# Two transformer blocks in one kernel: operands before squares at the seam, and two units evicted ahead of the norm's root

## The reference

```python
# first_block, its end
h2 = rmsnorm(x, norm_ffn)
gate, up = jnp.split(h2 @ w_ffn_in, 2, axis=-1)
x = x + (jax.nn.silu(gate) * up) @ w_ffn_out          # w_ffn_out: 2816 x 1024
x = rmsnorm(x, norm_final)
# second_block, its start
a = rmsnorm_2(x, norm_pre_mix)
proj = a @ w_in                                        # 1024 x 1960
...                                                    # gates, mLSTM, latent attention
mix = ...
x = x + rmsnorm_2(mix, norm_post_mix)                  # x is needed again here
```

## Time and profile before

| | us |
|---|---|
| median of 3 runs | 2873.16 |
| lowest and highest | 2871.89, 2873.46 |
| the profiled execution | 2871.33 |
| its span | 2869.6 |
| TensorE's mean granted clock in it | 0.986 |

### The profile page before, as it was taken

The page is one execution under the profiler, slowest core; times in us unless marked ns, Lnnn a source line. Parts: engine busy times, 40 slices in busy tenths (PEclk is TensorE's granted clock), DMA queues, the critical chain, the costliest instruction groups (busy, mean ns, idle before and its releaser), DMA issues.

```text
span 2869.6 us, 32978 instructions
## 1 busy us (share of the span) xinstructions
PE 2764.7 (96%) x12578; PEld 2186.6 (76%) x12578; DVE 1812.8 (63%) x2070; ACT 1021.9 (36%) x1397; POOL 1277.2 (45%) x780
## 2 busy tenths in 40 slices
PE   6999999999998999999998999999998999999998
PEld 5888688787776888887786887666577688878777
DVE  3111355655746766669878758666646766687877
ACT  4000233333214333334444014555545433344444
POOL 2433222223435888884333434101432788833331
PEclk9999999999999999999999999999799999999999
DMA  5222232324442333346631534002343355564543
GB/s 178 95 95 91 102 112 94 118 89 157 144 139 66 111 108 94 90 125 211 203 114 48 185 118 123 17 32 79 104 132 103 103 162 158 160 218 161 159 135 132
DMA packets 336967, 348.90 MB, mean 122 GB/s; under 512 B 18915, under 2 KB 256602, under 8 KB 336822
## 3 DMA queue, kind: packets, MB, share of 16 engines
q1 hardware_dynamic: 327254, 311.30, 35.2%
q10 hardware_dynamic: 9568, 35.66, 3.1%
HBM read 237.53 MB, written 108.34 MB: 121 GB/s over the span
## 4 chain that ended last, share of the span: by engine, by line
PE 78%; DVE 11%; issue 3%; DMA 3%; ACT 3%; POOL 1%; SPq 1%; DVEq 0%; ACTq 0%; POOLq 0%
PE ps L3264 34%; PE ps L532 29%; PE ps L2352 2%; PE ps L2374 2%; DVE op_lo L3341 2%; PE ps L939 1%; PE ps L2722 1%; DMA op_raw<-hidden 1%; PE ps L2362 1%; DVE sw_lo L3174 1%; PE ps L920 1%; PE ps L574 1%; PE ps L873 1%; PE ps L568 1%; PE ps L2840 1%
## 5 line engine op out<-in xcount | busy, mean ns | idle before, releaser
L3264 PE MATMUL ps<-op_hi,sw_hi 128*128 128x512 f32 x1769 | 693.5, 392 | 21.9 <-ACT s_p L3273 9.1
L3264 PE MATMUL ps<-op_lo,sw_hi 128*128 128x512 f32 x1769 | 690.2, 390 | 0.0
L3264 PE MATMUL ps<-op_hi,sw_lo 128*128 128x512 f32 x1769 | 690.1, 390 | 0.0
L498 POOL TENSOR_TENSOR w_hi_t<-w_raw,ones 128x1024 fp32r<-128x1024 f32 (+1 forms) x85 | 163.3, 1924 | 745.6 <-PE ps L532 356.4
L3264 PEld LDWEIGHTS ps<-op_hi,sw_hi 128*128 128x128 f32 x1769 | 333.2, 188 | 102.6 <-issue 17.3
L3264 PEld LDWEIGHTS ps<-op_hi,sw_lo 128*128 128x128 f32 x1769 | 333.2, 188 | 69.4
L3264 PEld LDWEIGHTS ps<-op_lo,sw_hi 128*128 128x128 f32 x1769 | 333.2, 188 | 69.0 <-issue 0.5
L655 DVE TENSOR_TENSOR stage<-ps,rstd 128x1024 f32<-128x1024 f32 x62 | 75.8, 1222 | 346.4 <-PE ps L532 328.0
L3164 ACT ACTIVATE sw_hi<-sw_sumNone 128x512 fp32r<-128x512 f32 (+1 forms) x252 | 157.1, 624 | 332.9 <-PE ps L3264 251.1
L532 PE MATMUL ps<-h1hi,w_hi_t 128*128 128x512 f32 x720 | 233.7, 406 | 14.6 <-DVE h1lo L616 10.6
L3174 POOL TENSOR_TENSOR sw_lo<-sw_sumNone,sw_hi 128x512 fp32r<-128x512 f32 x138 | 213.8, 1559 | 34.9 <-ACT sw_hi L3164 34.8
(11 more groups left out here) (441 smaller groups left out, 4935.9 us busy)
## 6 DMA issues: line engine op xcount, KB each, us to landing
op_raw<-hidden SPq DMA_DIRECT2D x42, 1024.0 KB, 8.6
w_raw<-in_w_in SPq DMA_DIRECT2D x60, 512.0 KB, 3.9
sw_raw<-in_w_ffn_in SPq DMA_DIRECT2D x44, 512.0 KB, 5.3
proj<-stage ACTq DMA_DIRECT2D x42, 512.0 KB, 2.6
hidden<-hidden_blocks SPq DMA_DIRECT2D x13, 1536.0 KB, 6.2
acc<-proj SPq DMA_DIRECT2D x36, 512.0 KB, 4.5
hidden<-hidden_blocks SPq DMA_DIRECT2D x14, 1280.0 KB, 5.0
sw_raw<-in_w_up SPq DMA_DIRECT2D x32, 512.0 KB, 8.3
```

The source lines that it names most:

```text
L498: ins = pool.tensor_tensor(whi[:, u.par, s], raw[:, u.par, s], ones[:, 0:1].to_broadcast([P, n]), ALU.mult)
L3264: mm = pe.matmul(out, w, x[:, k, :], start=(k == 0 and i == 0 and r < 4), stop=(k == n - 1 and i == 2), skip_group_check=r >= 4)
```

## The change

The order of operands and squares changes in and behind the last pair. Before, the tiles n = 4 and 5 of `FIN` were squared in the last pair and added in it and right behind it. Now n = 4 is still squared in the last pair, its sums and those of n = 5 to 7 come behind all eight operands, and the operands begin inside the last pair (`fin_hi` 0 to 2, `fin_lo` 0 to 2). Units 0 and 1 of the projection both run before the sums over features. Since `rstd` isn't there when they are done, ACT copies them out of their banks as they are (`unit_as_is`), and DVE multiplies them by `rstd` in `stage` later (`unit_root`), from where they are stored (`rooted_act`). The spread moves from unit 1 to unit 2, `fin_dve` and the spill from behind unit 0's store to behind unit 1's, and a `memset` on POOL from j = 2 to j = 4.

```diff
--- before.py
+++ after.py
@@ -244,7 +244,7 @@
          "h_mixed": ("o_gate", 16), "op_hi": ("o_hi", 8), "op_lo": ("o_lo", 8), "y_gained": ("sc_ready", 8),
          "out_row": ("kdt_ready", 8), "x3_squared": ("g_step", 24), "x3_summed": ("conv_step", 16), "qk_high": ("yb_ready", 8),
          "qk_low": ("yb_scaled", 8), "s_masked": ("o_sum", 8),
-         "x3_last_spilled": ("mv_loaded", 64)}
+         "x3_last_spilled": ("mv_loaded", 64), "unit_rooted": ("z_ready", 8)}
 LATER_PAIRED = {"sw_landed": ("gab_loaded", (128, 128)), "hid_stored": ("o_back", (80, 16)),
                 "x3_back": ("x_loaded", (16, 16)), "x3_spilled": ("x1_spilled", (64, 64))}
 OPERANDS = (("r_loaded", 64), ("v_loaded", 64), ("qk_loaded", 128), ("o_stored", 96), ("u_loaded", 64),
@@ -1644,11 +1644,14 @@
                     change_act(act, p, i)
                     if p < P1O and p % 2 == 0 and i in (3, 4, 5):
                         silu_act(act, p // 2, i - 3)
-                    if P1_LAST - 3 < p and i in (1, 4):
+                    if P1_LAST - 3 < p and i == 1 or P1_LAST - 3 < p < P1_LAST and i == 4:
                         fin_squares(act, 2 * (p - P1_LAST + 2) + i // 4)
+                    if p == P1_LAST and i == 4:
+                        for n in range(3):
+                            fin_hi(act, n)
                 if p < P1O and p % 2 == 0:
                     silu_act(act, p // 2, 3)
-            for n in range(KT):
+            for n in range(3, KT):
                 fin_hi(act, n)
 
         def gate_post(dve, p, what):
@@ -1736,10 +1739,9 @@
                 f1_in_dve(dve, p)
             for p in range(P1O, P2):
                 output_dve(dve, p)
-            fin_lo(dve, 3)
-            for n in range(4, KT):
+            for n in range(3, KT):
                 fin_lo(dve, n)
-            for n in (KT - 2, KT - 1):
+            for n in range(KT - 4, KT):
                 fin_add(dve, n)
 
         def f1_in_dve(dve, p):
@@ -1818,13 +1820,32 @@
                 dve.tensor_tensor(ssqB[:, :], ssqB[:, :], sqb_[:, :], ALU.add).then_inc(S["fin_done"], 1)
 
         def fin_act(act):
-            for n in (KT - 2, KT - 1):
+            for n in range(KT - 3, KT):
                 fin_squares(act, n)
+            for j in range(2):
+                unit_as_is(act, Step(U_IN2 + j))
             f = 2 * NORM_AT["final"]
             act.wait_ge(S["norm_sum"], f + 3)
             act.activation(r1, PS[2][:, :], ACT.Sqrt).then_inc(S["rstd_ready"], 1)
             act.wait_ge(S["norm_sum"], f + 4)
             act.activation(rstd[:, :], PS[3][:, :], ACT.Sqrt).then_inc(S["rstd_ready"], 1)
+
+
+
+        def unit_as_is(act, u):
+            act.wait_ge(S["unit_done"], u.times(1, 1))
+            act.wait_ge(S["stored"][u.par], 16 * stores_before(u, U_IN2, B2))
+            act.activation(stage[:, u.par, :], PS[u.par][:, :], ACT.Copy).then_inc(S["unit_out"][u.par], 1)
+
+        def unit_root(dve, u):
+            dve.wait_ge(S["unit_out"][u.par], u.nth())
+            dve.tensor_tensor(stage[:, u.par, :], stage[:, u.par, :], rstd[:, :], ALU.mult)\
+               .then_inc(S["unit_rooted"], 1)
+
+        def rooted_act(act, j, dst):
+            u = Step(U_IN2 + j)
+            act.wait_ge(*count("unit_rooted", j + 1))
+            act.dma_start(dst, stage[:, u.par, :]).then_inc(S["stored"][u.par], 16)
 
         def in2_weights_pool(pool, i):
 
@@ -1929,8 +1950,8 @@
             for j in range(N_IN2):
                 if j >= 2:
                     split_unit(pool, Step(U_IN2 + j))
-                if j == 2:
-                    pool.wait_ge(S["unit_done"], U_IN2 + 2)
+                if j == 4:
+                    pool.wait_ge(S["unit_done"], U_IN2 + 3)
                     pool.memset(cb[:, :, 0:3], 0.0).then_inc(S["ml_consts"], 1)
 
         def in2_pe(pe):
@@ -1941,8 +1962,8 @@
                             pe.wait_ge(S["lo_ready"], OPERAND["mix2"] + FIN.index(k) + 1))
                 else:
                     mm_unit(pe, Step(U_IN2 + j), g1hi, g1lo,
-                            wait_k=(lambda k: fin_spread(pe) if k == 3 else None) if j == 1 else None)
-                if j == 0:
+                            wait_k=(lambda k: fin_spread(pe) if k == 3 else None) if j == 2 else None)
+                if j == 1:
                     fin_pe(pe)
                 if j == 8:
                     pe.wait_ge(S["g_step"], 3 * C - 1)
@@ -1964,8 +1985,11 @@
         def in2_act(act):
             for j in range(N_IN2):
                 t = IN2_ORDER[j]
-                store_act(act, Step(U_IN2 + j), proj2[t * P:(t + 1) * P, :])
-                if j == 0:
+                if j < 2:
+                    rooted_act(act, j, proj2[t * P:(t + 1) * P, :])
+                else:
+                    store_act(act, Step(U_IN2 + j), proj2[t * P:(t + 1) * P, :])
+                if j == 1:
                     spill2_act(act)
                 if j == 2:
                     gates_act(act)
@@ -1999,8 +2023,11 @@
         def in2_dve(dve):
             dve.wait_ge(S["rstd_ready"], NORM_AT["mix2"] + 1)
             for j in range(N_IN2):
-                store_dve(dve, Step(U_IN2 + j), U_IN2, B2)
-                if j == 0:
+                if j < 2:
+                    unit_root(dve, Step(U_IN2 + j))
+                else:
+                    store_dve(dve, Step(U_IN2 + j), U_IN2, B2)
+                if j == 1:
                     fin_dve(dve)
                 if j == 3:
                     gates_dve(dve)
@@ -3622,8 +3649,10 @@
             else:
                 post(3, n2, H2, 3)
             next_lo(dve, p, 3)
-            if P1_LAST - 3 < p < P2:
+            if P1_LAST - 3 < p < P1_LAST:
                 fin_add(dve, 2 * (p - P1_LAST + 2))
+            if p == P1_LAST:
+                fin_lo(dve, 0)
             if N_PAIR - 4 < p:
                 end_adds(dve, p - 1)
             change_dve(dve, p, 4)
@@ -3632,6 +3661,8 @@
                 dve.tensor_copy(acc[:, n1, H1], bank(p, 4)).then_inc(S["s_post"], 1)
             else:
                 post(4, n1, H1, 0)
+            if p == P1_LAST:
+                fin_lo(dve, 1)
             next_lo(dve, p, 4)
             if fresh_sum:
                 post_sum(dve, p, "21", acc[:, n2, H1])
@@ -3645,8 +3676,7 @@
                 end_rows(dve, 0, 2)
             next_lo(dve, p, 5)
             if p == P1_LAST:
-                for n in range(3):
-                    fin_lo(dve, n)
+                fin_lo(dve, 2)
             change_dve(dve, p, 6)
             if fresh_sum:
                 post_sum(dve, p, "12", acc[:, n1, H2])
```

## The result

The changed kernel is slower: 2881.93 us, median of 7 executions (2878.53 to 2883.8), against 2873.16 us, also of 7, for the kernel before: ratio 1.0031, 95% interval 1.0021 to 1.0041. Measured again beside the experiments it was 2881.4 against 2873.66 us, ratio 1.0024 (1.0013 to 1.0034). Of all executions one was a slow one (3742.82 us at a mean granted clock of 0.689, of the first kernel with the gates' loads later); the ratio of that kernel leaves it out, its median does not. The profiled execution took 2881.93 us, its span is 2880.2 us.

A forecast was written before the change was run, and what follows sets the result against it. It took the start of the spill, whose chain of waits leads to unit 5, as the bound. Spill lateness +3.35 and restart +2.9 sum to +6.2 us on 2873.2: 2879.4 us, range 2873.5 to 2882.5.

The forecast's parts named there:

- What bounds the kernel: Before unit 5, the chain through spill, SP's loads and unit 5's weights binds, not PE; the spill's start counts.
- Operands: In unit 0, PE starts right behind the last product and waits 1.5 + 0.5 + 0.5 us for operands.
- The adds just hidden: Under unit 1, the adds of squares end at 1566.5 against unit 1's end at 1566.3; a slip beyond 1 us shows.
- Rival C: Before the sums, adds end 1 to 3 us after unit 1 and PE waits: +7 to +9 us; chance 0.17.
- The spread 2.2 us later: In unit 2, the spread comes at 1574.15 instead of 1571.94, 2.2 us later.
- The additional multiply 1.14: On DVE ahead of `fin_dve`, two multiplies instead of one cost 1.14 us more, making the spill 3.35 us late.
- Rival D: At `fin_dve`, POOL's split of unit 4 misses it, so it takes some 9.6 us: +2.3 us, 2875.4; chance 0.05.
- The rest of the chain costs what it cost: From spill to unit 5, spill, SP's loads, load and split cost as before; unit 5 can start at 1618.45.
- PE's stand 12.7 us: Between units 4 and 5, PE stands still for 12.7 us and its clock falls to the lower level.
- The restart 2.9 us: From unit 5, PE's slow restart loses 2.9 us, the middle of three earlier restarts; bounds 1.5 to 4.3.
- rival B: At unit 5, chain late by 2 to 3.3 us, short restart (1.5): +3.5 to +4.9 us, within noise; chance 0.26.
- Rival A: At unit 5, weights are there when PE comes, so it starts 9.4 us earlier: 2863.8 us; chance 0.10.

The follow-up runs named there:

- the first kernel with the gates' loads later: Changed kernel with SP's gates' loads behind unit 7's weights instead of unit 4's, gates' work on ACT moved later by the simplest edit: 2879.28 us, ratio 1.0017.
- PE kept busy: Changed kernel plus fifty matmuls into a free bank between units 4 and 5, results unread: 2881.52 us, ratio 1.0029.
- the operands alone: Changed kernel with sums back behind unit 0, spread in unit 1, banks left to DVE and the root; only operand order differs from before: 2877.61 us, ratio 1.0019.
- the root behind: Changed kernel with the two additional multiplies by rstd and their stores put behind the final-norm multiplies and the spill: 2883.12 us, ratio 1.0038.
- the units alone: Changed kernel with operands and squares in the order of before, units 0 and 1 still ahead of the sums: 2890.53 us, ratio 1.0055.

## Why the prediction was right

Forecast 2879.4 us, measured 2881.93, inside the range but 0.6 us below its upper end; and slower by more than 0.2%, to which the text gave 0.45, as much as to no difference. The mechanism was right, and the size of the total in part luck: the seam came out a little shorter than forecast, and 2.2 to 3.3 us came from stages that the sum had left out. By its steps, the times of after aligned:

- *What bounds the kernel* (when the spill starts): shown. The chain of waits after names it, and moving SP's stand with all that hangs on it turned a loss of 8 us into a gain of 7 (2867.23), where the same edit was worth nothing on the kernel before.
- *Operands*: unit 0 close behind the last product (forecast within 0.5 us, measured 0.23 us from start to start), then 1.5 us for operand 1: measured 1.51. The other two waits were charged at 0.5 us each; one pair of matmuls starts 0.76 us after another there, instead of 0.454, so each is 0.3. Unit 1's end was forecast at 1566.3, the sums start at 1566.19.
- *The adds just hidden* (end 1566.5): they end at 1563.47, aligned 1566.40, and the second sum starts 1.57 us after that. Rival C, adds as the wait, is out.
- *The spread 2.2 us later*: 1573.85 against 1571.94, 1.9.
- *The additional multiply 1.14*, spill 3.35 later: 2.36 us for two multiplies; the final norm's eight took 13.43 again, as taken; aligned the spill starts at 1594.28, 3.04 later. Rival D, a faster `fin_dve`, is out.
- *The rest of the chain costs what it cost*: true in the sum and not in its parts. The spill took 13.29 us instead of 11.78 (+1.5), SP's small loads 2.61 instead of 3.21 (-0.6), the load and split of unit 5 8.48 instead of 8.85 (-0.4). Unit 5 starts at 1618.68 aligned; forecast 1618.45.
- *PE's stand 12.7 us*: 12.03. Unit 4 began late: its first pair of matmuls starts at 1592.60, 1.01 us after the pair before it instead of 0.454, since the eviction of unit 2 (L655), which empties its bank, stands behind `fin_dve` on DVE.
- *The restart 2.9 us*: the term that was mis-sized. The windows give (1 - 0.80) x 10.00 = 2.0 us, and PE kept busy took 1.2 to 1.9 us off the seam. The bounds of 1.5 to 4.3 held. That the middle row followed the longest of three gaps was no reason to choose it: gaps of 12.0, 11.34 and 5.52 us cost 2.0, 2.9 and 2.9 us in the runs here, and one of 8.4 cost 2.9 in the earlier trace rows, so the length of a gap doesn't order the prices.

The Trainium skill, TensorE: Matmul & The Clock Gate (Terms), puts the penalty at the throttled time by one minus the granted share; the slow pairs here (1.22 and three of 1.05 us where 0.62 is usual) run from 1615.75 to about 1619.6, and half of 3.9 us is 1.9: the trace agrees.

So the seam was forecast 6.2 us longer and is 5.5 longer (mean of 5.1, 5.6 and 5.8). That lies between the forecast and rival B (3.5 to 4.9): the chain was as late as in the forecast, the restart nearly as short as in B. The medians differ by 8.8 us, and by 7.7 in the second measurement; the terms of the sum have no place for the remaining 2.2 to 3.3 us. By the table they are in the mLSTM (+2.4 in the mean of three profiles, against -0.1 for the further profiles of before) and the heads (4.8 against 2.3 in the mean of four), less 1.8 in what lies ahead of the seam and in the MLP. That was a missing term: the prediction took everything after unit 5 as fixed because PE is busy there without a hole, but a busy PE is not a PE at full clock.

What stays open is why. The late unit 5 isn't it: the mLSTM was 2.1 us longer in the kernel before with the gates' loads moved, whose seam was not late, and 2.6 longer where the seam was 8.9 us shorter; and it was 1.0 us shorter with the operands alone. Three values near -1.0, -0.1 and +2.1 to +2.6, with the clock's share moving with them (0.86 for after, 0.89 for before, 0.91 with the operands alone), point to which waits in the stage fall into a slow stretch, but no experiment set it on purpose. That it isn't chance alone is shown by the repeats: four profiles of before within 0.1 us of each other, three of after within 0.4 us. For the heads, chance between executions is shown (0 and +3.1 for one kernel, +2.7 and +5.9 for the other), a shift of the mean by the change is not.

Rival A, unit 5's weights there in time, was rejected for the right reason. Made true by moving SP's loads and all that hangs on them, it gave 6.8 us less than the kernel before (2867.23 against 2874.01); its price had been worked out as 9.4 less.

## What to carry to other kernels

Before repairing gaps on the busiest engine, find the next place where it meets another chain, and compare arrival times: here they were 0.1 us apart, so 9 us won on PE were worth nothing until the queue in between was reordered, and the reordering alone was worth nothing either. A DMA queue that waits on one transfer holds every later load, however little that load has to do with it. When such a queue's wait is moved, move every consumer's due time with it, or the next one gives the gain back.

## What the runs showed of the hardware

**A large store that ends on one engine.** The spill of 4 MB took 11.8 us in all four profiles of the kernel before, with the operands alone and with the root behind (12.0 in the kernel before with the gates' loads later), and 13.3 or 13.7 in the changed kernel (three profiles), with the units alone, with PE kept busy, and in the changed kernel with either order of later gates' loads. DMA view of after, 1591 to 1605 us (busy tenths and GB/s in 40 slices, then packets by queue):

```profile
DMA  0004999999999999999999999999999999996000
GB/s 0 0 0 176 398 433 386 410 374 410 398 456 386 398 398 398 421 398 421 386 398 433 363 398 421 398 445 410 386 421 374 445 433 386 374 433 258 23 23 35
...
q10 hardware_dynamic: 1181, 4.71, 84.4%
q8 instruction: 1, 0.02, 0.4%
```

With the operands alone, 1590.5 to 1603 us:

```profile
DMA  0000599999999999999999999999999999999999
...
q10 hardware_dynamic: 1122, 4.53, 90.5%
```

In after the last slices run at 23 to 35 GB/s, about a sixteenth of the 400 before them. The last packets follow each other one at a time, where 16 were under way before, so I read it as one of the 16 engines that still writes when the others are done. One packet of instructions (queue q8) lies among the spill's packets in all seven profiles that took 13.3 us or more, and in none of the seven others. That the one delays the other is a reading of this coincidence and was not tested. Of its 1.5 us in the first profile of after 0.5 reached unit 5, because SP's loads and unit 5's load and split came out 1.0 us shorter.

**The clock between executions.** One kernel's stage of 34 to 37 us differs by 3.1 us from one execution to the next with PE's idle time the same (2.9 us), only a mean granted clock of 0.95 or 0.86. For changes of a few us the stages outside the edit have to be compared one by one before the total is believed.
